# First attention of a two-block transformer kernel: a key load moved in SyncE's queue, and ScalarE and VectorE work moved from tile ends to single steps

## The reference

```python
h = rmsnorm(x, g_mix)
z = h @ w_in
zb, zc, zx, zq, zk, zv = split(z)                 # 6 x 512 columns
y_c = zb * causal_dwconv3(zc * zx, conv_w, conv_b)
q = rmsnorm(zq per head); k = rmsnorm(zk per head); v = zv     # 8 heads of 64
y_a = dilated_attention(q, k, v)
y = concat([rmsnorm(y_c), rmsnorm(y_a)])
x = x + y @ w_out

def causal_dwconv3(u, w, b):
    return up[:, 0:t] * w[0] + up[:, 1:t + 1] * w[1] + up[:, 2:t + 2] * w[2] + b
```

## Time and profile before

| | us |
|---|---|
| median of 3 runs | 2587.83 (2584.77 to 2589.29) |
| the profiled execution | 2583.64 |
| its span | 2582.0 |
| PE busy in the span | 2516.0 (97%) |
| DVE, ACT, POOL busy | 1361.7, 1055.3, 1265.2 |
| DMA queue of the DMAs that SP issues | 244 MB, 27.9% of 16 engines' span |
| chain that ended last | PE 87%, DVE 4%, ACT, DMA, POOL and issue 2% each, SP's queue 1% |

### The profile page before, as it was taken

One profiled execution on the slowest core, in us unless ns is written; L12 is line 12 of the kernel. 1 busy time (PEld: TensorE's weight loads), 2 busy tenths in 40 slices (PEclk: granted clock), 3 DMA queues, 4 the chain that ended last, 5 costly groups with the idle time before them and its releaser, 6 DMA issues.

```text
span 2582.0 us, 34606 instructions
## 1 busy us (share of the span) xinstructions
PE 2516.0 (97%) x12210; PEld 2088.5 (81%) x12210; DVE 1361.7 (53%) x2479; ACT 1055.3 (41%) x1951; POOL 1265.2 (49%) x940
## 2 busy tenths in 40 slices
PE   8989999999999999999999999889999999999999
PEld 6877878888888888888877777689888888888887
DVE  5327766188766762225267888777247333333222
ACT  6336653253333332224256666586234333322120
POOL 2122323457766665534525554454356666656441
PEclk9999999999999999999999999999999999999999
DMA  4253432312222244210323212320412222226311
GB/s 157 75 170 117 116 82 83 146 58 106 90 82 88 77 160 175 82 65 27 107 74 94 66 62 70 108 69 21 155 74 74 82 85 79 82 105 222 114 45 70
DMA packets 107402, 246.28 MB, mean 95 GB/s; under 512 B 18880, under 2 KB 40672, under 8 KB 106976
## 3 DMA queue, kind: packets, MB, share of 16 engines
q1 hardware_dynamic: 107232, 244.08, 27.9%
HBM read 184.27 MB, written 55.05 MB: 93 GB/s over the span
## 4 chain that ended last, share of the span: by engine, by line
PE 87%; DVE 4%; ACT 2%; issue 2%; DMA 2%; POOL 2%; SPq 1%; ACTq 0%; DVEq 0%; POOLq 0%
PE PS L965 10%; PE PS L964 10%; PE PS L963 10%; PE PS L701 8%; PE PS L703 8%; PE PS L702 8%; PE PS L981 6%; PE PS L982 6%; PE PS L983 6%; PE PS L1233 2%; PE PS L1213 1%; PE PS L806 1%; PE PS L933 1%; PE PS L935 1%; PE PS L934 1%
## 5 line engine op out<-in xcount | busy, mean ns | idle before, releaser
L701 PE MATMUL PS<-Hh,Wl 128*128 128x512 f32 x1072 | 434.3, 405 | 12.0 <-DVE Hl L1364 9.4
L703 PE MATMUL PS<-Hh,Wh 128*128 128x512 f32 x1072 | 420.7, 392 | 0.0
L702 PE MATMUL PS<-Hl,Wh 128*128 128x512 f32 x1072 | 420.3, 392 | 0.0
L3220 POOL TENSOR_TENSOR Wl<-Wr,Wh 128x512 fp32r<-128x512 f32 (+1 forms) x158 | 209.4, 1346 | 336.0 <-ACT Wh L2320 335.7
L3323 POOL TENSOR_TENSOR RG<-RW,RG 128x512 fp32r<-128x512 f32 x176 | 246.9, 1408 | 130.2 <-ACT RG L2631 130.0
L1807 DVE TENSOR_TENSOR XA<-PS,XA 128x512 f32<-128x512 f32 x192 | 132.4, 691 | 332.5 <-PE PS L983 332.5
L981 PE MATMUL PS<-Hh,RG 128*128 128x512 f32 x704 | 274.1, 389 | 1.6 <-POOL Hl L3419 1.2
L983 PE MATMUL PS<-Hh,RG 128*128 128x512 f32 x704 | 273.9, 389 | 0.0
L982 PE MATMUL PS<-Hl,RG 128*128 128x512 f32 x704 | 273.9, 389 | 0.0
L3323 POOL TENSOR_TENSOR RG<-SW,RG 128x512 fp32r<-128x512 f32 x120 | 165.3, 1377 | 171.5 <-ACT RG L2631 147.0
L965 PE MATMUL PS<-Hh,RG 128*128 128x512 f32 x640 | 249.0, 389 | 0.0
(11 more groups left out here) (365 smaller groups left out, 5145.6 us busy)
## 6 DMA issues: line engine op xcount, KB each, us to landing
RW<-in_wg SPq DMA_DIRECT2D x44, 512.0 KB, 3.7
RW<-in_wu SPq DMA_DIRECT2D x44, 512.0 KB, 4.6
R<-in_wd SPq DMA_DIRECT2D x88, 256.0 KB, 3.0
hgscr<-GB SPq DMA_DIRECT2D x44, 512.0 KB, 2.6
G<-hgscr SPq DMA_DIRECT2D x40, 512.0 KB, 6.8
Wr<-in_wi SPq DMA_DIRECT2D x27, 512.0 KB, 3.4
Wr<-in_wo SPq DMA_DIRECT2D x16, 512.0 KB, 3.3
spill<-X SPq DMA_DIRECT2D x16, 512.0 KB, 2.6
```

What stands on the lines that cost most here:

```text
L701: pe.matmul(ps(b), k.Wl[:, s, wc], xh[:, kx, sl], start=kk == 0, stop=False)
L702: pe.matmul(ps(b), k.Wh[:, s, wc], xl[:, kx, sl], start=False, stop=False)
L703: i = pe.matmul(ps(b), k.Wh[:, s, wc], xh[:, kx, sl], start=False, stop=kk == nk - 1)
L3220: i = pool.tensor_tensor(k.Wl[:, s, c], k.Wr[:, s, c], k.Wh[:, s, c].bitcast(F32), ALU.subtract)
```

## The change

It has six parts.

- SP: `key_load(1)` is issued ahead of the sixteen value stores, and no longer in step 0 of head 0.
- ACT: the copy of the next head's keys is split in two halves of 512 columns, at i = 3 and i = 4, and `next_head(s)` comes behind the exponential of the same step.
- ACT: `use()`, so the weights' high part, is called at kk 2 of a unit's first tile (behind the unit's first attention step), no longer ahead of the tile.
- DVE: for j < 3 the first term of the convolution moves from the end of tile (x, 1) to kk 2 of (b, 0), the taps to kk 6 of (b, 0) and kk 2 of (b, 1), the products with B to kk 4 of (b, 1) and kk 2 of the next unit's first tile. j = 3 stays.
- ACT and POOL: the squares of conv tile j, half 0 and 1, and their sums move to the end of tile (b, 1) and to the first tile of the next unit (ACT at its kk 6, POOL at its end).
- SP: the store of conv tile j moves from behind unit (j, b) to behind the first tile of the next unit, among the steps of `tables1()`.

```diff
@@ DVE
         dve.tensor_tensor(zs, ps(b), zs, ALU.mult).then_inc(*up(("free", b), "zx", j, half))
-        if half == 0:
-            return
+
+    def conv_first(j):
         y = k.YC[:, j % 2, :]
...
-                taps = {2: lambda j=j: conv_tap(j, 1), 6: lambda j=j: conv_tap(j, 0)} if (c, half) == ("b", 0) else {}
-                walk(8, 2, taps, tick)
+                later = {}
+                if (c, half) == ("c", 0) and j:
+                    later = {2: lambda j=j, b=b: conv_b(j - 1, 1, b)}
+                if (c, half) == ("b", 0):
+                    if j < 3:
+                        later = {2: lambda j=j: conv_first(j), 6: lambda j=j: conv_tap(j, 1)}
+                    else:
+                        later = {2: lambda j=j: conv_tap(j, 1), 6: lambda j=j: conv_tap(j, 0)}
+                if (c, half) == ("b", 1) and j < 3:
+                    later = {2: lambda j=j: conv_tap(j, 0), 4: lambda j=j, b=b: conv_b(j, 0, b)}
+                walk(8, 2, later, tick)
...
+                    if (j, half) == (3, 1):
+                        conv_first(3)
                 if c == "b":
-                    conv_b(j, half, b)
                     if j == 3:
+                        conv_b(j, half, b)
@@ ACT
     def key_high(h):
-        act.wait_ge(*at("k1_in", h, 1))
-        act.activation(k.KSa[h % 2][:, :], k.KSr[:, :], ACT.Copy).then_inc(*up("q_hi", "k1_hi", h))
+        key_part(h, 0)
+        key_part(h, 1).then_inc(*up("q_hi", "k1_hi", h))
+
+    def key_part(h, z):
+        if z == 0:
+            act.wait_ge(*at("k1_in", h, 1))
+        return act.activation(k.KSa[h % 2][:, half_of(z)], k.KSr[:, half_of(z)], ACT.Copy)
...
+        if i == 3 and h < 7:
+            key_part(h + 1, 0)
         if i == 4 and h < 7:
-            key_high(h + 1)
+            key_part(h + 1, 1).then_inc(*up("q_hi", "k1_hi", h + 1))
...
-            if s < n:
-                next_head(s)
             if 1 <= s <= n:
...
+            if s < n:
+                next_head(s)
...
+    def conv_square(j, half):
+        staged = [("v2_in", 0, 7), ("v_kept", 7)] if (j, half) == (1, 0) else []
+        square("conv", j, half, k.YC[:, j % 2, half_of(half)], staged + [("yb", j, half)])
...
-            use()
             for half in range(2):
-                walk(8, 2, {}, tick)
+                later = {}
+                if half == 0:
+                    later[2] = use
+                if (c, half) == ("c", 0) and j:
+                    later[6] = lambda j=j: conv_square(j - 1, 1)
+                walk(8, 2, later, tick)
                 b = bank.next()
+                if (c, half) == ("b", 1) and j < 3:
+                    conv_square(j, 0)
@@ POOL
-                if c == "b" and 0 < j < 3:
-                    add("conv", j, half)
-                    pool.wait_ge(*at("acc", "conv", half, j))
+                if (c, half) == ("b", 1) and 0 < j < 3:
+                    add("conv", j, 0)
+                    pool.wait_ge(*at("acc", "conv", 0, j))
+                if (c, half) == ("c", 0) and 0 < j - 1 < 3:
+                    add("conv", j - 1, 1)
+                    pool.wait_ge(*at("acc", "conv", 1, j - 1))
@@ SP
-            if i == 0 and h < 7:
+            if i == 0 and 0 < h < 7:
                 key_load(h + 1)
...
     sp.dma_start(k.rr[:, :], d["T1"][0]).then_inc(*up("d_tab", "tab", 0))
+    key_load(1)
     for i in range(8):
...
+                if (c, half) == ("c", 0) and j:
+                    sp.wait_ge(*at("yb", j - 1, 1))
+                    sp.dma_start(d["yscr"][j - 1], k.YC[:, (j - 1) % 2, :]).then_inc(
+                        *up(("d_ys", j - 1), "yc_stored", j - 1))
...
-        if j < 3:
-            sp.wait_ge(*at("yb", j, 1))
-            sp.dma_start(d["yscr"][j], k.YC[:, j % 2, :]).then_inc(*up(("d_ys", j), "yc_stored", j))
```

More of the change, by code:

```diff
@@ L2599, in scalar @@
         for c in "cxb":
-            use()
             for half in range(2):
-                walk(8, 2, {}, tick)
+                later = {}
[4 more added lines that the diff above has]
+                walk(8, 2, later, tick)
                 b = bank.next()
+                if (c, half) == ("b", 1) and j < 3:
+                    conv_square(j, 0)
                 if c == "b":
-                    staged = [("v2_in", 0, 7), ("v_kept", 7)] if (j, half) == (1, 0) else []
-                    square("conv", j, half, k.YC[:, j % 2, half_of(half)], staged + [("yb", j, half)])
                     if j == 3:
+                        conv_square(3, half)
                         y_high(half)
```

## The result

The changed kernel takes 2606.16 us (2604.18 to 2610.27, 4 runs), the kernel before 2588.56 (2584.77 to 2589.59, 4 runs): a ratio of 1.0073, 95% interval 1.0055 to 1.0090, so slower by 0.7%. The forecast for the median was 2604, 2.2 us too low. The profiled execution took 2604.18 us, its span 2602.7; for it the sum had 2600.6, 3.6 too low.

What follows compares the result with a forecast made beforehand. The prediction took TensorE (PE), busy 97% of the span, to bound the kernel. Won parts -21.9, late loads +32.9 and clock +6 gave +17.0 us, so 2604 us on the median; range 2578 to 2620.

Steps and rivals of the forecast that it cites:

- The chain through SP's queue: Heads 1 to 7: weights copy 3.9 us later delays POOL, SP's fetch and loads queued behind; query waits 2.9 us each.
- The key term: Heads 1 to 6: first key half, at step 3, waits for its load; late 5.0 us a head, query's 2.9 included.
- the clock: PE at half clock around the two waits per head: 0.85 us a head, 6 us lost, bounds 0 and 24.
- (a): Before head 1: its keys loaded ahead of the stores remove a 7.57 us stall and half clock; 8.7 us won (6.7 to 9.7).
- The charge for late stores: First attention steps: ACT's first probability copies wait for values stored later; 0.5 us (0 to 1.5) off the win.
- (b): Heads 1 to 7: reordered exponential, taps, first conv step and squares remove PE's waits; all 11.7 us won.
- The terms at nothing: Halved key copies, moved DVE work, held bank, POOL sums, conv tile's store, weights in units 8 to 11: priced at about 0.
- (c): Tail of attention: PE's waits behind L1453 and L1433, some 2 us together, of which 1.5 go (0 to 2).
- The first: Heads 1 to 7: only the query waits, key copies find loads landed; 20.3 us plus clock 2, 2588 us; chance 0.12.
- The second: Heads' loads land before they bite much: no key waits, queries 1.0 us sooner, 13.3 us lost; 2579 us; chance 0.07.
- the third: The weights' one-step delay stays hidden within SP's slack; only the 21.9 us win remains, 2566 us; chance 0.09.
- The fourth: PE's clock falls in every head by the long stretch, 24 us: +35 in all, 2623 us; chance 0.08.

Runs made afterwards that it cites:

- experiment 2: Kernel before with only ACT's weights copy moved behind a unit's first attention step: 2618.8 us, ratio 1.0122.
- experiment 3: Changed kernel with SP's weight fetch moved behind SP's own first attention step, weights copy left as changed: 2566.5 us, ratio 0.9920.
- experiment 4: Changed kernel with the two halves of the key copy one step later, at steps 4 and 5: 2600.2 us, ratio 1.0045.
- experiment 5: Kernel before with only the keys of head 1 loaded ahead of the sixteen value stores: 2581.6 us, ratio 0.9982.
- experiment 10: Changed kernel with SP's fetch behind its first step, key copy at steps 4 and 5, head 1's keys behind four tiles' stores: 2562.8 us, ratio 0.9903.
- experiment 1: Changed kernel with ACT's weights copy back at a unit's start, all else as changed: 2581.4 us, ratio 0.9977.
- experiments 9 and 10: The first is experiment 10 plus the weights copy back at the unit's start: 2563.2 us, ratio 0.9904; the second is experiment 10 itself.

## Why the prediction was right, step by step

**The chain through SP's queue** held in each link, in the trace after and by experiments 2 and 3. The query waits of PE in step 3 were 2.84, 2.76, 3.42, 3.26, 2.63, 2.14 and 2.92 us in the seven heads, 20.0 in sum; the prediction had 7 x 2.9 = 20.3.

**The key term and the clock** came out right in sum and differently within. Predicted were 32.9 us of waits and 6 of clock, 38.9 over heads of 24.4; measured 209.3 - 170.8 = 38.5. But key waits were only 4.5 us and not 12.6. In heads 1, 2, 3 and 5 a stretch of 3.4 us at 0.50 began between 0.5 us ahead of the end of the query wait and 1.2 us behind it, and PE reached its second product late with 0.7 us of wait, or none, ahead of it. In head 1 that product was to be 4.3 us late in all; it came 2.84 late by the wait and 1.6 by half clock (4.10 us from product to product for 2.47 in the earlier trace rows), and no key wait was left. The prediction had put such a stretch at no cost since the keys land when they land; in head 1 it is the same 4.5 us, told as clock. Over the seven heads, 38.5 less 20.0 and 4.5 leaves 14.0: an estimated 10 from six stretches of 3.4 us at half clock (1.7 each), 0.7 of waits for low parts in heads 2 and 5, and some 3 that were not broken down. The experiment without key waits (4) shows the floor: the time at half clock grew from 20 us to 34, and only 6 us came back.

**Won parts.** (a) was mis-sized: from the first transposes to head 1 it took 18.9 us for 26.0, so 7.1 won and not 8.7. The 4.3 us at 0.50 behind the stall went with it: in the changed kernel the clock is 1.00 from 166 to 202.6 us. The charge for late stores was 0.5; PE's two waits behind them were 0.64 and 0.69, and by the starts of the transposes the two steps took 1.8 us more than before. In the queue the third tile's store took 4.96 us to issue for 2.36 before. The charge for the query load, 0.5, was wrong the other way: the load part alone (experiment 5) won 5.3 in this stretch, with a query wait of 2.0, and in the changed kernel, where the exponential stands ahead of the query copy, that wait is absent.

(b) was mis-sized too, and the sum hides it. With the loads in time and all else as changed (experiment 3) the seven heads took 174.2 us, so the change's new order won 182.5 - 174.2 = 8.3 and not 11.7. The rest came only with the key copy a step later (171.3 in experiment 10, against 170.8 as the most that could be won). The terms at nothing had priced the halved key copy but not its earlier step. (c) gave 1.3 us by the same matmuls, predicted 1.5.

**The sum.** Late loads then cost 209.3 - 174.2 = 35.1 us where 38.9 were forecast, and the won parts gave 7.1 + 8.3 + 1.3 = 16.7 for 21.9. The mechanism was right; that the total is this close is in part luck, since two errors of 4 to 5 us offset each other. -16.7 + 35.1 = +18.4 of the span's 20.7. Of the rest 1.3 us lie ahead of the first attention, where nothing changed: that start varied from 167.1 to 170.7 us between the runs. The last 1.0 lies behind the attention and was not looked into. By medians the change cost 17.6 us, and 17.0 were forecast.

**Rivals.** The first (keys find their load landed) is refuted by ACT's rows: all six first key halves were ended by their load, 13.9 us in sum. The second and third (loads in time) fell with the heads' length; with another order on SP the time is that of the third (2566.5 against its 2566). The fourth (long half clock in every head) did not come: six stretches of 3.4 us. In experiment 4 three of seven heads had it long, 6.8 us. The conv tile's store among a head's loads, which the prediction named as a risk, cost nothing that shows: heads 3 and 6 take 24.4 and 24.5 us in experiment 3.

**What stays open.** When the clock falls is not settled: head 6 had waits of 2.1 and 1.1 us and kept 1.00, head 7 one wait of 2.9 and 3.4 us at 0.50 from 0.2 us behind its end. In experiment 4 all seven single waits of 2.7 to 3.4 us had a stretch at 0.50 beside them, begun up to 1.2 us behind the wait's end or up to 1.0 ahead of it; in experiment 1 one wait of 3.8 had one (0.50 from 340.9 to 344.2) and one of 2.3 had none. In experiment 1 heads 2 and 6 took 28.3 and 30.1 us. Their key halves landed 7.4 and 7.7 us after issue (median of a head's two), those of the other heads 6.4 to 6.9; why these bursts are slower was not tried.

## What to carry to other kernels

Before a step is moved, list who waits for it on other engines, and then what is queued behind those waits: here a copy moved by 4 us on ScalarE won nothing (experiments 9 and 10) and cost 31 us (experiment 2), because in each of seven heads a fetch that waits for it stands in the queue ahead of the head's loads. Put the transfers that are due first ahead of a prefetch that waits for a buffer in the same queue: here that order was worth 40 us (experiment 3 against the changed kernel). Where a copy's row reads "idle <- DMA", its load had no slack: the query copy of head 1 stood 0.42 us before and 4.20 with the fetch ahead of its load issued 3.8 us later in the head, the key copy of head 3 stood 0.15 us before and 1.90 as a half copy a step earlier (experiment 1).

## What was not expected of the hardware

In these traces issuing a DMA was not of constant cost. With the two key loads ahead of the stores, the small store of the third tile held SP's queue for 4.96 us, without them for 2.36; in the changed kernel the other seven tiles' took 0.47 to 0.77. It is no accident of one execution: the six traces with the keys ahead have 4.4 to 5.0 us, the six without 1.9 to 2.5. What holds the issue was not tried. First the changed kernel, then the kernel before, both SP's timeline:

```profile
164.50 4.96 SPq L3715 DMA_DIRECT2D V<-VS  x1
```

```profile
162.34 2.36 SPq L3684 DMA_DIRECT2D V<-VS  x1
```

What stands behind that store was late by more than the issue time of the instructions put ahead: the key loads took 1.09 us to issue, and the fourth tile's store went 10.0 us behind the table load (160.10 to 170.14) for 6.7 before (158.72 to 165.38), 3.4 us later. And the waits came with more than their length: in six of the changed kernel's seven heads, waits of 2.6 to 3.4 us came with 3.4 us at a granted clock of 0.50, an estimated 1.7 us of PE's time.
